# An encoder step on one core: the tiles of u from a stride of 591 floats and a 32-byte start to a stride of 592 floats and a 64-byte start

## The reference

```python
def _swiglu(u, w_in, w_out):
    h = u @ w_in
    a, b = h[..., :D_FF], h[..., D_FF:]
    return (jax.nn.silu(a) * b) @ w_out

for i in range(DEPTH):                      # DEPTH = 2
    j = i // N_MIXERS
    x = x + 0.5 * _swiglu(_rmsnorm(x, norm_ffn1[i]), ffn1_w_in[i], ffn1_w_out[i])
    u = _rmsnorm(x, norm_mix[i])
    if i % N_MIXERS == 0:
        y, hist = _pool_mixer(u, pool_hist[j], pos0, pool_w[j], pool_b[j], pool_scale[j])
    else:
        y, (C, n, m) = _mlstm_mixer(u, mC[j], mn[j], mm[j], mlstm_w_in[j], mlstm_b_i[j], mlstm_b_f[j],
                                    mlstm_norm[j], mlstm_w_out[j])
    x = x + y
    x = x + 0.5 * _swiglu(_rmsnorm(x, norm_ffn2[i]), ffn2_w_in[i], ffn2_w_out[i])
return _rmsnorm(x, norm_final), ...
```

## Time and profile before

| | |
|---|---|
| median of three runs | 2054.7 us |
| lowest, highest | 2051.86, 2060.67 us |
| profiled execution | span 2056.6 us; the page names no other time for it |
| PE busy | 2031.3 us (99%), 14936 matmul instructions |
| DVE, ACT, POOL busy | 42%, 31%, 8% |
| granted TensorE clock, mean | 0.986 of 2.4 GHz |
| DMA | 24.5% of 16 engines on the main queue |

### The profile page before, as it was taken

How to read it: one execution, slowest core, us unless ns; L and a number is a source line. 1 busy time by engine, 2 the same in 40 slices (tenths; PEclk the granted TensorE clock), 3 DMA queues, 4 the chain that set the end, 5 groups by cost and what they waited for, 6 DMA issues and landing times.

```text
span 2056.6 us, 35068 instructions
## 1 busy us (share of the span) xinstructions
PE 2031.3 (99%) x14936; PEld 2012.8 (98%) x14936; DVE 859.8 (42%) x939; ACT 643.5 (31%) x787; POOL 172.9 (8%) x129
## 2 busy tenths in 40 slices
PE   8999999999999999999999999999999999999997
PEld 8999999999999999999999999999989999999997
DVE  7444433328444442344444433352545644443222
ACT  4333322125333321233333322232342433332111
POOL 4000001114000000110000001100013200000121
PEclk9999999998999999999999999999999999999998
DMA  4222222212222222222222222221112222222221
GB/s 151 82 82 82 82 77 85 78 59 70 85 82 82 82 79 85 82 76 88 82 82 82 79 78 84 77 97 58 62 42 82 83 82 82 82 82 77 85 79 52
DMA packets 47788, 164.14 MB, mean 80 GB/s; under 512 B 5681, under 2 KB 5697, under 8 KB 47729
## 3 DMA queue, kind: packets, MB, share of 16 engines
q1 hardware_dynamic: 46656, 160.87, 24.5%
q10 hardware_dynamic: 880, 2.20, 0.3%
q0 software_dynamic: 192, 0.20, 0.0%
HBM read 159.71 MB, written 3.53 MB: 79 GB/s over the span
## 4 chain that ended last, share of the span: by engine, by line
PE 96%; DVE 2%; ACT 1%; DMA 0%; issue 0%; POOL 0%; DVEq 0%; ACTq 0%
PE ps L1001 91%; DVE u_lo L686 1%; PE ps L1130 1%; PE ps L1246 0%; DVE w_lo L680 0%; PE ps L1249 0%; PE ps L1236 0%; PE ps L1144 0%; ACT w_hi L438 0%; DMA gains<-in_gains 0%; ACT u_hi L442 0%; PE ps L1205 0%; PE ps L1026 0%; DVE x L989 0%; PE ps L1217 0%
## 5 line engine op out<-in xcount | busy, mean ns | idle before, releaser
L1001 PE MATMUL ps<-u_hi,w_hi 128*128 128x288 f32 x3328 | 720.7, 298 | 3.2 <-DVE u_lo L686 2.1
L1001 PE MATMUL ps<-u_hi,w_lo 128*128 128x288 f32 x3328 | 720.8, 298 | 0.0
L1001 PE MATMUL ps<-u_lo,w_hi 128*128 128x288 f32 x3328 | 716.3, 297 | 0.0
L438 ACT ACTIVATE w_hi<-w_raw 128x1024 fp32r<-128x1024 f32 (+2 forms) x308 | 317.4, 1031 | 1114.3 <-PE ps L1001 1108.2
L1001 PEld LDWEIGHTS ps<-u_hi,w_hi 128*128 128x128 f32 x3328 | 543.7, 191 | 8.1 <-issue 3.8
L680 DVE TENSOR_TENSOR w_lo<-w_raw,w_hi 128x1024 fp32r<-128x1024 f32 (+2 forms) x308 | 407.1, 1322 | 340.6 <-ACT w_hi L438 340.5
L1001 PEld LDWEIGHTS ps<-u_hi,w_lo 128*128 128x128 f32 x3328 | 538.8, 190 | 0.0
L1001 PEld LDWEIGHTS ps<-u_lo,w_hi 128*128 128x128 f32 x3328 | 536.8, 190 | 0.0
L1001 PE MATMUL ps<-h_lo,w_hi 128*128 128x288 f32 x1408 | 301.5, 296 | 0.0
L1001 PE MATMUL ps<-h_hi,w_lo 128*128 128x288 f32 x1408 | 301.5, 296 | 0.0
L1001 PE MATMUL ps<-h_hi,w_hi 128*128 128x288 f32 x1408 | 301.4, 296 | 0.0
(11 more groups left out here) (186 smaller groups left out, 881.0 us busy)
## 6 DMA issues: line engine op xcount, KB each, us to landing
w_raw<-in_ffn_in SPq DMA_DIRECT2D x176, 512.0 KB, 3.3
w_raw<-in_ffn_out SPq DMA_DIRECT2D x64, 512.0 KB, 3.5
w_raw<-in_ffn_out SPq DMA_DIRECT2D x32, 384.0 KB, 3.2
w_raw<-in_mlstm_in SPq DMA_DIRECT2D x24, 512.0 KB, 3.3
w_raw<-in_mlstm_out SPq DMA_DIRECT2D x8, 512.0 KB, 3.3
out_y<-x SPq DMA_DIRECT2D x8, 288.0 KB, 2.9
x<-in_x SPq DMA_DIRECT2D x6, 288.0 KB, 7.3
w_raw<-in_pool_w SPq DMA_DIRECT2D x4, 256.0 KB, 2.6
```

Of the source, the lines that this page charges most:

```text
L438: act.activation(w_hi[:, n % RING, 0:size], w_raw[:, n % RAW, 0:size], ACT.Copy) \
L1001: mm = pe.matmul(ps[:, bank + h, 0:HALF], w, m[:, h * HALF:(h + 1) * HALF], start=first and p == 0, stop=last and p == 2)
```

## The change

A constant `U_STRIDE` is 592, the next multiple of 16 above 591. u_hi and u_lo get rows of that length, and the allocator is moved up to a multiple of 64 bytes ahead of them. The last float of each row is not used. No instruction is added, removed or moved.

```diff
@@ -31,6 +31,7 @@
 D_FF = 2816
 FT = D_FF // P
 HIST = 15
+U_STRIDE = (TOK + HIST + 15) // 16 * 16
 GROUPS = 4
@@ -85,7 +86,8 @@
     x = sb("x", [P, DT, TOK])
 
-    u_hi, u_lo = sb("u_hi", [P, DT, TOK + HIST], F32R), sb("u_lo", [P, DT, TOK + HIST], F32R)
+    place[0] = (place[0] + 63) // 64 * 64
+    u_hi, u_lo = sb("u_hi", [P, DT, U_STRIDE], F32R), sb("u_lo", [P, DT, U_STRIDE], F32R)
     scratch = place[0]
     h_hi, h_lo = sb("h_hi", [P, FT, TOK], F32R), sb("h_lo", [P, FT, TOK], F32R)
     scratch_end = place[0]
```

## The result

The changed kernel takes 2042.95 us (median of five runs, 2040.72 to 2044.18), the kernel before 2054.7 us (five runs, 2051.86 to 2060.67). The ratio is 0.9934, 95% interval 0.9921 to 0.9948: 0.66% or 11.75 us less, about three times the forecast of 4.2 us. The profiled execution took 2044.18 us with a span of 2042.1 us, so some 2.1 us lie around the span.

The account below looks back on a forecast made before the run. PE's gapless matmul stream was taken as the bound; 4.1 us from matmuls on u plus 0.1 us from ACT and DVE gave 4.2 us off the 2054.7 us median, so 2050.5 us, range 2042 to 2058.

Parts of the forecast that it names:

- What bounds the kernel: PE, busy 99% of the span, mostly block_mm's matmuls at L1001; its largest group of waits is 2.6 us.
- the 0.41 ns: Excess of each L1001 matmul reading u (133.75 ns) over one reading h (133.34 and 133.33 ns), ascribed to u's addresses.
- the excess isn't the addresses: Rival for L1001 matmuls on u: alignment changes nothing, time stays 2054.7 us; chance 0.10.
- a period of 1.2 GHz for each read off an 8-byte pair: Matmul reads of u: 0.83 ns lost by each starting mid-pair, 24 of 48 matmuls per project.
- Within the class of 64-byte starts u becomes what h is: L1001 matmuls: with every u row on 64 bytes, u takes h's pace, 133.33 ns.
- the upper bound of 4.2 us: Most that the matmuls on u could gain, taking the pace on aligned h as limit.
- the third rival: Aligned u beats h on L1001 by reads in groups of four floats: 12.5 us, 2042.2 us; chance 0.09.
- matmuls on u: Term for 9984 matmuls of L1001 at 0.41 ns less each: 4.1 us less, all on the path.
- Everything behind u moves by 64 bytes: Term for h and weights, whose positions to one another stay: taken as 0, bounds 11.8 us each way.
- ACT, DVE, weight loads from u: Terms for instructions on u outside L1001: 0.1 us for ACT and DVE, 0 for pool-stage weight loads.
- aligned u becomes faster than h: Rival for L1001: one four-float group fewer in 3/4 of 9984 matmuls, 12.5 us, 2042.2 us; chance 0.09.
- The move modulo 128 costs: Rival: moving read and next weight load collide in 14208 matmuls, +7.6 us net, 2062.3 us; chance 0.04.

Follow-up runs that it names:

- e1: Kernel before, rows still 591 floats, with u_lo started on 64 bytes and everything behind it placed as in the changed kernel: 2051.03 us, ratio 0.9979.
- e10: Changed kernel with u rows of 576 floats like h, history left out, repeated in ten executions: 2049.3 us, ratio 0.9969.
- e2: Kernel before with 64 unused bytes added behind u_lo, u itself unmoved: 2053.75 us, ratio 0.9986.
- e3: Changed kernel with 64 unused bytes ahead of the weight tiles, first run: h pace 132.23 ns; no time of this run is given.
- e4: Changed kernel with u rows of 576 floats like h, history left out, first and single run: 2041.26 us.

## Why the prediction was right and wrong

- **What bounds the kernel**: right. PE without a gap, every nanosecond of pace on the path: the paces of u give 12.9 us, the spans differ by 14.5, and part of the rest is in where the clock fell. No wait took its place; PE's largest groups of waits stayed at 2 to 3 us.
- **That the 0.41 ns were addresses**: right. e1 takes exactly these away without touching an instruction, and the rival "the excess isn't the addresses" is out. But it needed no 64-byte rows for this, only another start of u_lo (0.27 ns) and of what follows (0.14 ns).
- **How the 0.41 ns were explained**, a period of 1.2 GHz for each read off an 8-byte pair: wrong. It fitted three numbers (20 ns per project, 13 ns in the gates' unit, 24 of 48 matmuls) by chance. In e1 as many rows as before begin off 8 bytes, and the excess is gone; at step 578 no row does, and 0.14 ns of it is there.
- **"Within the class of 64-byte starts u becomes what h is"**: this is the step that failed, and with it the upper bound of 4.2 us: h was taken as the floor for u. Two layouts count as one class only if everything that sets the pace is equal. With h's step u does become h (133.33, e10). With 592 it doesn't (132.22 or 132.78): the rows of u stand at four places modulo 256 where those of h stand at one, and against the weights at two distances modulo 128. I named the first difference under the third rival and took h for the floor all the same. The term "matmuls on u" was forecast at 4.1 us and measured 12.9.
- **"Everything behind u moves by 64 bytes", taken as 0**: 1.4 us less by pace (e2). The reason given, that positions to one another stay, holds for h and the weights but not for u, which doesn't move with them. That h would keep its pace, because h and weights keep their distance, was right (133.34), and e2 and e3 together show that this reason is the true one.
- **ACT, DVE, weight loads from u**: 0.1 us was forecast. ACT's u_hi went from 775 and 688 to 774 and 686 ns, DVE's u_lo from tmp from 751 to 749:

```profile
L444 ACT ACTIVATE u_hi<-x,gains 128x576 fp32r<-128x576 f32 x48 | 36.2, 774 | 122.1 <-DVE x L740 112.2 <-DVE x L777 5.9 <-DVE x L973 3.0
```

  The unmoved tmp from x (762 ns before) has 760, still 14 ns less than the now aligned u_hi. So the 13 to 19 ns between rows weren't alignment. The 30 matmuls of the pool stage in the earlier trace rows take 3.60 us, unchanged.
- **The rivals**: "aligned u becomes faster than h" came out, with 2042.2 us against 2042.95 measured, and it had a chance of 0.09. Its size is near by luck, for its mechanism isn't what the runs show: if one group of four floats fewer were the gain, step 576 would have it. "The move modulo 128 costs" named the right quantity, the distance of moving rows to weights, and the wrong sign. The measured time is inside the range, near its lower end; the chances were not right, with 0.89 on "within 0.5%".

What stays open: what in the chip ties the pace to these places, why the place of a row and its neighbours' act together, and why one layout can have two paces (132.22 and 132.78 at step 592; 133.33 and, once, 130.0 at step 576). No run here tells a clash of the two reads from another cause that depends on addresses. Weights' places other than multiples of 32 bytes weren't tried.

## What to carry to other kernels

Where PE streams without a gap, measure its pace (length over count of a piece of the chain) for each operand's layout, and expect about 1% between layouts: here it followed from the step of the moving rows and their distance to the weight blocks together. Equal alignment doesn't make two layouts equal; take one as the other's bound only if their steps, and their distances to the weights, are the same, and even then allow for a second pace. Padding the step and shifting the weights are one-line trials, and worth trying in pairs, since one can take back what the other gives.

## What was not expected of the hardware

- Equal matmuls of 288 columns on equal 128 x 128 weights ran at steady paces from 130.0 to 133.75 ns at full clock, with PE never waiting: by their addresses, and for two layouts also by stage or execution.
- 64 bytes more ahead of the weight tiles: h from 133.33 to 132.22 ns; with 32, 96 or 128 bytes h stays at 133.33.
- A pace is kept through a whole stage and over unit and loop borders (200 us for 1540 matmuls at 130.0 ns, and the following 120 us too), and the same program may have another in the next stage or execution.
- The difference isn't spread evenly. On h at 133.33 ns (changed kernel, third FFN) three of twelve intervals between matmul starts are 140 ns and the others 130 to 132; in the FFN at 130.0 ns (e4) they are 128 and 132 in turn.
